# Turning the expert tokens on VectorE instead of TensorE, and loading w_down in blocks of whole rows, in a hybrid encoder layer with sixteen experts

## The reference

```python
aff = softmax(tok @ router_w)                 # tok: (512, 1024) of one sequence, 16 experts
gate, idx = lax.top_k(aff.T, 64)              # each expert takes its 64 best tokens
xs = tok[idx]
hid = silu(xs @ w_gate[e]) * (xs @ w_up[e])   # w_gate, w_up: (1024, 1408) for each expert
ye = (hid @ w_down[e]) * gate                 # w_down: (1408, 1024)
out = zeros.at[idx].add(ye)                   # added to the tokens' residual
```

## Time and profile before

| what | value |
|---|---|
| median of three runs | 1491.75 us (1491.37 to 1493.68) |
| profiled execution, from first to last instruction | 1489.4 us |
| mean granted TensorE clock | 0.996 |
| TensorE, VectorE, ScalarE, GpSimd busy | 99%, 80%, 55%, 11% of the span |
| the expert stage | about 712 to 1478 us |
| one expert, from block 0 to the next block 0 | 47.8 us |

### The profile page before, as it was taken

The page is one execution under the profiler, slowest core; times in us unless marked ns, Lnnn a source line. Parts: engine busy times, 40 slices in busy tenths (PEclk is TensorE's granted clock), DMA queues, the critical chain, the costliest instruction groups (busy, mean ns, idle before and its releaser), DMA issues.

```text
span 1489.4 us, 18913 instructions
## 1 busy us (share of the span) xinstructions
PE 1467.0 (99%) x7042; PEld 1235.5 (83%) x7042; DVE 1189.5 (80%) x1024; ACT 819.8 (55%) x777; POOL 167.3 (11%) x119
## 2 busy tenths in 40 slices
PE   9999999999999999998999999999999999999996
PEld 8878888888888888888888888888888888888885
DVE  5688988896767766346888888888888888888886
ACT  6322232123622222333677777777777777777776
POOL 1000001000005200011110112011110121012101
PEclk9999999999999999999999999999999999999998
DMA  7210232623263255677999999999999999999997
GB/s 236 58 43 0 81 87 75 224 85 99 94 230 121 87 183 197 227 253 283 347 362 365 376 376 374 384 374 377 374 377 381 377 374 374 384 376 376 374 374 286
DMA packets 220971, 388.26 MB, mean 261 GB/s; under 512 B 8603, under 2 KB 87771, under 8 KB 220412
## 3 DMA queue, kind: packets, MB, share of 16 engines
q1 hardware_dynamic: 213692, 361.39, 68.4%
q0 software_dynamic: 7232, 26.22, 5.8%
HBM read 348.78 MB, written 38.80 MB: 260 GB/s over the span
## 4 chain that ended last, share of the span: by engine, by line
PE 71%; DVE 2%; DMA 0%; issue 0%; ACT 0%; POOLq 0%; POOL 0%; ACTq 0%
PE ps L1779 23%; PE ps L1781 22%; PE ps L1780 22%; PE ps L2162 1%; PE ps L2154 1%; PE ps L2199 1%; PE ps L2082 0%; PE ps L2064 0%; DMA slot_tokens<-tok_rows,rows_to_gather 0%; DVE top_index L1651 0%; DVE affinity_rows L1654 0%; DVE top_of_halves L1647 0%; DVE expert_lo L1207 0%; DVE tok_rows L1592 0%; ACT expert_hi L804 0%
## 5 line engine op out<-in xcount | busy, mean ns | idle before, releaser
L1207 DVE TENSOR_TENSOR expert_lo<-expert_raw,expert_hi 128x2048 fp32r<-128x2048 f32 (+1 forms) x285 | 597.5, 2110 | 92.1 <-ACT expert_hi L804 91.1
L804 ACT ACTIVATE expert_hi<-expert_raw 128x2048 fp32r<-128x2048 f32 (+1 forms) x285 | 506.5, 1778 | 177.8 <-PE ps L1781 174.0
L1779 PE MATMUL ps<-expert_hi,slot_tokens_T_hi 128*128 128x512 f32 (+1 forms) x768 | 289.8, 377 | 2.0 <-DVE slot_tokens_T_lo L1207 1.0
L1780 PE MATMUL ps<-expert_lo,slot_tokens_T_hi 128*128 128x512 f32 (+1 forms) x768 | 285.2, 371 | 0.0
L1781 PE MATMUL ps<-expert_hi,slot_tokens_T_lo 128*128 128x512 f32 (+1 forms) x768 | 285.2, 371 | 0.0
L1779 PE MATMUL ps<-hT_hi,w_hi 128*128 128x512 f32 x576 | 226.2, 393 | 1.0 <-DVE hT_lo L1219 1.0
L1781 PE MATMUL ps<-hT_hi,w_lo 128*128 128x512 f32 x576 | 224.3, 389 | 0.0
L1780 PE MATMUL ps<-hT_lo,w_hi 128*128 128x512 f32 x576 | 224.2, 389 | 0.0
L1779 PEld LDWEIGHTS ps<-expert_hi,slot_tokens_T_hi 128*128 128x128 f32 x768 | 144.1, 188 | 25.1 <-issue 4.0
L1781 PEld LDWEIGHTS ps<-expert_hi,slot_tokens_T_lo 128*128 128x128 f32 x768 | 144.2, 188 | 20.4
L1241 DVE SCALAR_TENSOR_TENSOR conv_sum<-a_padded,small_params,conv_sum 128x1024 f32<-128x1024 f32 x120 | 158.1, 1317 | 3.4
(11 more groups left out here) (314 smaller groups left out, 1843.6 us busy)
## 6 DMA issues: line engine op xcount, KB each, us to landing
expert_raw<-in_w_gate SPq DMA_DIRECT2D x64, 1024.0 KB, 8.7
expert_raw<-in_w_up SPq DMA_DIRECT2D x64, 1024.0 KB, 8.6
expert_raw<-in_w_down SPq DMA_DIRECT2D x64, 1024.0 KB, 8.1
expert_raw<-in_w_gate SPq DMA_DIRECT2D x32, 768.0 KB, 7.5
expert_raw<-in_w_up SPq DMA_DIRECT2D x32, 768.0 KB, 7.2
expert_raw<-in_w_down SPq DMA_DIRECT2D x32, 768.0 KB, 8.5
w_raw<-in_w_in SPq DMA_DIRECT2D x36, 512.0 KB, 4.8
gate_in<-gate_spill SPq DMA_DIRECT2D x22, 512.0 KB, 3.9
```

The source lines that it names most:

```text
L804: nc.scalar.activation(out, src, ACT.Copy, **scale).then_inc(s, 1)
L1207: V.tensor_tensor(out, src, high_part.bitcast(F32), ALU.subtract).then_inc(s, 1)
L1779: nc.tensor.matmul(out, a[0], b[0], start=first, stop=False)
L1780: nc.tensor.matmul(out, a[0], b[1], start=False, stop=False)
```

## The change

It has four parts.

1. **Tokens of experts 1 to 15.** The gather becomes four indirect DMAs of a quarter row (256 channels) each; the row numbers differ by quarter of the partitions, from a new table `PIECES` made once in the routing stage (four small ScalarE copies, four small TensorE transposes, one VectorE operation, four more VectorE memsets earlier). VectorE then turns `XS` with one transpose of 128x1024 in squares of 32, reading every eighth element, into the new buffer `TURNED` after its part of block 8 (`turn_tokens`). ScalarE's high part comes ahead of its part of block 0 and waits until block 15 of the expert before has been used. The low part is made by GpSimd (`tokens_low`). The eight TensorE transposes stay for expert 0 alone.
2. **Row order.** The channels of a tile are now every eighth, so gate and up are loaded with eight neighbouring rows in a partition instead of rows 128 apart. The pieces stay 2 KB or 1.5 KB long.
3. **`w_down`.** A block is two row tiles with all 1024 columns. Blocks 10, 11, 16, 17 keep their size; 4 and 5, equal before, become 128x2048 and 128x1024. TensorE goes through both column halves tile by tile. `gate_out` waits for both blocks.
4. **Order elsewhere.** The load of the last norm's weights moves from the routing stage to the end of the weight loads. GpSimd's `scatter` of an expert comes one turn later in its program, after the gather of the expert after next.

```diff
 def src_of(kind, c, k, e):
     if kind == "down":
-        tiles = n // P
-        return w_down[bass.ds(e, 1), a:a + n, k * 512:(k + 1) * 512].rearrange(
-            "o (t p) n -> p (o t) n", p=P), tiles, 512
+        tiles, _ = place_of(kind, c, k)
+        a += 2 * k * P
+        return w_down[bass.ds(e, 1), a:a + tiles * P, :].rearrange("o (t p) n -> p (o t) n", p=P), tiles, D
     w = w_gate if kind == "gate" else w_up
-    return w[bass.ds(e, 1), k * 4 * P:(k + 1) * 4 * P, a:a + n].rearrange(
-        "o (t p) n -> p (o t) n", p=P), 4, n
+    return w[bass.ds(e, 1), :, a:a + n].rearrange(
+        "o (p t) n -> p (o t) n", p=P)[:, 4 * k:4 * k + 4, :], 4, n
 def place_of(kind, c, k):
-    return (n // P, 512) if kind == "down" else (4, n)
+    return (min(2, n // P - 2 * k), D) if kind == "down" else (4, n)
...
+            sp.wait_ge(xsT_lo, E)
+            sp.dma_start(NGF[:], norm_f_g.to_broadcast([P, D])).then_inc(norm_g_in, 16)
             sp.wait_ge(added, 16 * (E - 1))
...
 def gather(e):
+    pool.wait_ge(xs_in, (e - 1) * 64 + 16)
+    ge(pool, xs_turned, e)
+    pool.wait_ge(slots_ready, 5)
+    nc.gpsimd.tensor_copy(NEXT_PIECES[:], PIECES[:, bass.ds(e, 1), :].rearrange("p o a -> p (o a)")).then_inc(rows_next, 1)
     pool.wait_ge(x2_mm, WO_DONE)
     pool.wait_ge(rows_next, e)
-    pool.indirect_dma_start(XS[:], None, tok_dram,
-                            bass.IndirectOffsetOnAxis(ap=NEXT_ROWS[:], axis=0)).then_inc(xs_in, 16)
+    for a in range(4):
+        pool.indirect_dma_start(XS[:, a * 256:(a + 1) * 256], None, tok_pieces,
+                                bass.IndirectOffsetOnAxis(ap=NEXT_PIECES[:, a:a + 1], axis=0)).then_inc(xs_in, 16)
+def tokens_low(e):
+    pool.wait_ge(xsT_hi, e + 1)
+    nc.gpsimd.tensor_tensor(XST[1][:].rearrange("p k n -> p (k n)"), TURNED[:].rearrange("p k n -> p (k n)"),
+                            XST[0][:].rearrange("p k n -> p (k n)").bitcast(F32), ALU.subtract).then_inc(xsT_lo, 1)
...
-            with pool.Fori(1, E - 1) as e:
+            with pool.Fori(2, E - 1) as e:
+                tokens_low(e)
                 gather(e + 1)
-                scatter(e)
+                scatter(e - 1)
...
 def xsT_high(e):
-    act.wait_ge(xsT_mm, e + 1)
-    high(XST[0][:].rearrange("p k n -> p (k n)"), PS[:, 6:8, :].rearrange("p a n -> p (a n)"), xsT_hi)
+    act.wait_ge(xs_turned, e + 1)
+    act.wait_ge(e_used, e * NB - SKIPPED - len(down_units(1)))
+    high(XST[0][:].rearrange("p k n -> p (k n)"), TURNED[:].rearrange("p k n -> p (k n)"), xsT_hi)
 def act_body(e, base, first, last=False):
     for n in range(NB):
+        if n == 0 and not first:
+            xsT_high(e)
         if not (first and LEAD <= n < LEAD + SKIPPED) and not (last and n == NB - 1):
             split_e(n, e, base)
...
+def turn_tokens(e):
+    dve.wait_ge(xs_in, e * 64 + 16)
+    dve.wait_ge(xsT_lo, e)
+    V.transpose(TURNED[:], XS_BY_TILE).then_inc(xs_turned, 1)
+TURN_AT = 8
 def dve_body(e, base, first, last=False):
     for n in range(NB):
...
-        if n == (1 if first else 0):
-            xsT_low(e)
+        if first and n == 1:
+            first_tokens_low()
...
+        if n == TURN_AT and not last:
+            turn_tokens(e + 1)
...
 def pe_body(e, base, first, last):
...
     else:
-        tokens_of(e + 1)
         down(1, e, down_counts(1, e, base))
+        hidden_T(2, e)
         pe.wait_ge(xsT_lo, e + 2)
-        hidden_T(2, e)
```

More of the change, by code:

```diff
@@ L1087, in split_e @@
                 q = pos_mod(n, e, SPLITS)
-                high(ES[q][:, 0:tiles, 0:width], EW[r][:, 0:tiles, 0:width], e_hi)
+                high(block_of(ES[q], *BODY[n]), block_of(EW[r], *BODY[n]), e_hi)
             def silu(c, e, base):
@@ L1120, in gate_out @@
                     act.wait_ge(slots_ready, 3)
-                    act.wait_ge(e_used, used + dh)
+                    act.wait_ge(e_used, used + 1)
                     ge(act, added, e * 16)
@@ L1134, in act_body @@
                             nc.scalar.activation(LISTS[:, g, 0, :], TOP[32 * g:32 * g + E, :], ACT.Copy).then_inc(rows_ready, 1)
-                    if n == (2 if first else 0):
+                    if first and n == 2:
+                        act.wait_ge(pair_ready, 1)
+                        for a in range(4):
+                            part = nc.scalar.activation(FOUR_TIMES[:, a, :, :], PAIR[:, 1, 32 * a:32 * a + 32][:, None, :].to_broadcast([E, 4, P // 4]),
+                                                        ACT.Copy)
+                        part.then_inc(rows_ready, 1)
+                    if first and n == 2:
                         xsT_high(e)
@@ L1567, in _ @@
                 steps.did(V.memset(HALF_START[32 * g:32 * g + 32, :], float(H * g)))
+                steps.did(V.memset(QUARTER[32 * g:32 * g + 32, :], float(g)))
             def row_scale(t):
@@ L2148, in _, with slot_pieces @@
             nc.tensor.transpose(PS[:, 0, 0:E], PAIR[:, 0, :], IDENT[0:E, 0:E]).then_inc(slots_mm, 1)
+            def slot_pieces():
+                pe.wait_ge(rows_ready, 6)
+                for a in range(4):
+                    mm = nc.tensor.transpose(PS[:, 4, a * E:(a + 1) * E], FOUR_TIMES[:, a, :, :].rearrange("e b n -> e (b n)"),
+                                             IDENT[0:E, 0:E])
+                mm.then_inc(slots_mm, 1)
             def tokens_of(e):
@@ L2224, in pe_body @@
                     hidden_T(2, e)
-                    down_whole(HIDT_WHOLE, 4, 1, E * NB - SKIPPED - 1, False)
+                    landed(E * NB - SKIPPED - 1)
+                    for dh in range(2):
+                        for tile in (2, 3):
+                            mm = down_whole(HIDT_WHOLE, tile, dh, E * NB - SKIPPED - 1, 1, 1, False)
+                    mm.then_inc(e_used, 1)
                 else:
-                    tokens_of(e + 1)
                     down(1, e, down_counts(1, e, base))
+                    hidden_T(2, e)
                     pe.wait_ge(xsT_lo, e + 2)
-                    hidden_T(2, e)
             keep_busy(22)
+            slot_pieces()
             tokens_of(0)
@@ L2239, in _ @@
             pe.wait_ge(hidT_hi, NF * E + 1)
+            end_tiles = (F - 2 * 512) // P
+            for pair in range(2):
+                landed(E * NB - SKIPPED + pair)
             for dh in range(2):
-                down_whole(HIDT_END, (F - 2 * 512) // P, dh, E * NB - SKIPPED + dh, True)
+                for tile in range(end_tiles):
+                    mm = down_whole(HIDT_END, tile, dh, E * NB - SKIPPED + tile // 2, NF - 1, tile // 2, tile == end_tiles - 1)
+                mm.then_inc(e_used, 1)
 def kernel(**inputs):
```

104 lines of the change are left out of this document (57 added, 47 removed).

## The result

The changed kernel takes **1523.13 us** (median of 4 runs, 1522.92 to 1523.22) against 1491.89 us for the kernel before on the same chip (4 runs): ratio 1.0208, 95% interval 1.0193 to 1.0222, so 31 us slower. The forecast was 1502.8 us, in a range of 1484 to 1521. The sign was right. The size was nearly three times too small, and the range missed it by 2 us.

What follows compares the result with a forecast made beforehand. The prediction took TensorE's queue (99% busy) as the bound. It summed 15 x (-0.31 + 0.30 + 0.64) = +9.5 us and +1.5 us once to +11.0 us on 1491.75: 1502.8 us, range 1484 to 1521 us.

Steps and rivals of the forecast that it cites:

- Block 16: Removing the eight TensorE transposes ahead of block 16 saves 0.31 us per expert, 15 times, not their full 0.80.
- Block 0: GpSimd's subtraction holds up VectorE's low part of block 0, so TensorE loses 0.30 us per expert, 15 times.
- Block 9: Later low parts plus VectorE's transpose delay TensorE at block 9: 0.64 us lost per expert, 15 times.
- the shift by block 4: Block 4 with 12 matmuls instead of 9 delays ScalarE's parts of blocks 7 and 8 by 0.46 us.
- The upper bound (2.44 us): Longest assumed VectorE transpose ahead of block 9: two passes of 1.22 us, losing 1.86 us there.
- rival (c): VectorE's transpose ahead of block 9 takes two passes: +29.3 us, 1521.0 us; chance 0.13.
- its 19 us more: With the skill page's 2.49 us for VectorE's transpose, block 9 loses 1.91 us and the whole takes 19 us more.
- What occurs once: Single costs such as routing-stage work and the first gather: 0 to 3 us, taken as 1.5 us.
- Rival (d): Gathers land late, or the new row order slows the loads by over 5%: from 1510 us up; chance 0.07.
- Rival (a): VectorE fits both new operations in its gaps, leaving only the 0.31 us saving: 1488.6 us; chance 0.22.
- gives nothing back: VectorE's subtraction of 1024 columns after block 0 saves nothing when removed, as VectorE ran ahead of TensorE there.
- the lag that the prediction named: Loads need 48.6 us per expert against 47.8 us for one expert; the ring covers 12 us of lag.

Runs made afterwards that it cites:

- run 2: Changed kernel with the tokens' low part made by VectorE after its part of block 17, no GpSimd subtraction; 1514.4 us.
- run 3: Changed kernel with w_down in the old blocks (half the columns, all row tiles); 1516.3 us.
- run 4: Changed kernel with VectorE's transpose reading neighbouring elements instead of every eighth; does not compute the layer; 1508.5 us.
- run 11: Changed kernel with one gather of whole rows per expert instead of four of quarter rows; does not compute the layer; 1517.5 us.
- run 5: Changed kernel with VectorE's transpose after block 12 instead of 8 and the tokens' low part on VectorE after block 17, none on GpSimd; 1487.0 us.
- run 7: Kernel before with only w_down's new blocks of two row tiles of 1024 columns; 1491.5 us.
- run 1: Changed kernel with VectorE's transpose after its part of block 12 instead of block 8; 1495.8 us.
- run 8: Kernel before with one TensorE token transpose instead of eight per expert from the second on; does not compute the layer; 1490.9 us.
- run 9: Kernel before with w_down's new blocks, one token transpose, unturned tokens read from SBUF, TensorE's wait for their low part behind the hidden state's transposes; 1489.9 us.
- run 6: Changed kernel with the transpose after block 12, the tokens' low part on VectorE, and w_down's old blocks; 1492.4 us.

## Why the prediction was off, point by point

- **Block 16, right.** Forecast -0.31 us. From block 9 to block 16 it is now 1001.90 + 49.43 - 1033.91 = 17.42 us, before 1036.39 - 1018.64 = 17.75: -0.33. TensorE stands 0.17 us there; the forecast said about 0.3.
- **Block 0, right in kind, short in size.** Forecast +0.30. From block 16 to block 0 it is 6.70 us against 6.22: +0.48. GpSimd's subtraction holds VectorE as in the earlier trace rows, and the hold was sized right: TensorE starts block 0 4.56 us after VectorE's low parts of blocks 16 and 17 end (1008.60 - 1004.04), the forecast said 4.53. The 0.18 us short are mostly that block 16 now comes 2.35 us after the start of its low part instead of the 2.50 of the forecast. Run 2 without the subtraction gives 0.59 back.
- **Block 9, the step that failed.** Forecast +0.64, measured 1.66 + 0.33 - 0.48 = +1.51. Of its two terms the shift by block 4 was right (0.46; run 3 shows 0.52). The other, "I take 1.22 us, one pass at the pace of the subtraction", was mis-sized: 2.17 us. Run 4 shows that the pace itself was right, 1.24 us when neighbours are read. What was left out is that `XS_BY_TILE` reads every eighth element, which stands in the diff. Putting 2.17 for 1.22 in the same sum gives +1.59, close to what was measured. The upper bound (2.44 us) held the value; rival (c), priced from it, comes to 1521.0 us, but for a reason that did not occur: there are no two passes whatever the step. That the time came out near this rival is luck.
- **The rule of the Trainium skill** that was weighed there ("VectorE: DVE Perf Modes", section "The three transpose paths", 2.49 us for eight, an estimate by the page) was nearer to the trace's 2.17 us than the row chosen, and its 19 us more would have given 1521.8 us. But it says nothing of the step, and with step one the transpose takes 1.24 us (run 4), half of the estimate: that it came near is luck as well. For TensorE's transposes the same section's 390 ns stands against 0.10 us each here.
- **What occurs once**, forecast 1.5 us: 4.3 at the first expert, -0.5 in the tail and 3.3 at the end, 7.1 us. The late first gather had been named ("its transpose may wait once") but not priced, the lower clock behind it not at all, and the end not thought of. Run 11 shows 3.6 us of the first expert and the 3.3 us at the end to come with the four gathers.
- The sum: 15 x 1.66 + 7.1 = 32.0 us against 15 x 0.63 + 1.5 = 11.0. Of the 21 us missing, 15 x 0.87 = 13 hang on block 9, 15 x 0.18 = 2.7 on block 0, and 5.6 on what occurs once; block 16 gave 0.3 more than forecast.
- **Rival (d)** did not occur from the second expert on: VectorE waits for a gather once. No run tests the row order of gate and up alone, but with it the transfers go at 382 GB/s (run 5) and without it at 384 (run 7), so it does not slow them by 5%. **Rival (a)** asked for a transpose under 0.6 us; the runs show another way to free block 9, a place in the queue where a long one is covered (run 1).
- Of the removed VectorE operation the prediction said that it "gives nothing back: it stood where VectorE ran ahead of TensorE". The reason is wrong: in the kernel before it ended 0.13 us before TensorE's next step that needed it (run 8). It gave nothing back in the changed kernel because block 0 waits there for its own low part behind GpSimd's hold. What its place alone is worth no run isolates; run 5, where it comes ahead of block 0's part, is 0.46 us per expert shorter than run 9, where it comes behind.

That TensorE was 99% busy made its work look like the price list. Run 8 shows that it was not: 0.7 us of it per expert were cover for a chain of VectorE that is as long. The change pays when that chain is put in another order too (run 5), and then the loads have to keep up as well (run 6): the lag that the prediction named, 48.6 us against 47.8, grows with a shorter expert.

## What to carry to other kernels

When work moves to an engine that is nearly full, ask in which gap of its queue it lands: the same 2.1 us transpose cost 24 us over 15 experts ahead of a late block and next to nothing four blocks on. Price an operation with its access pattern, not only with its size. And before counting on time taken off the busiest engine, look for the chain that ends next; here TensorE's work, VectorE's low parts and the loads came one closely behind the other.

## What the runs showed of the hardware that was not expected

- A VectorE transpose of 128x1024 fp32 takes 1.24 us when it reads neighbours (run 4) and 2.17 us when it reads every eighth element.
- SyncE's last wait for TensorE's queue is 5.4 us with four gathers per expert (5.6 in run 6) and 2.1 us with one. Why it follows their number is not known; no run tries two or three.
- TensorE's granted clock fell (0.57 from 736 to 740 us, at the 1.2 GHz level for most of it) behind an idle time of 3.18 us, and stayed at 1.00 in run 11 where the wait at the same place was 1.05 us. The length of the idle time is not all that counts: run 2 stood 3.09 us there and stayed at 1.00, run 4 stood 2.19 us and fell to 0.58 from 734 to 738 us. Run 2, then run 4:

```profile
736.28 0.50 PE L1817 MATMUL ps<-expert_hi,slot_tokens_T_hi 128*128 128x512 f32 x1 [3.09 <-DVE expert_lo L1230]
...
736.00:740.00 4.00, 3.72 (x16) 2.90 (x17) 4.00 (x4) 0.61 (x1) 3.12 (x2) 1.00 1.05 401
```

```profile
734.26 0.50 PE L1818 MATMUL ps<-expert_hi,slot_tokens_T_hi 128*128 128x512 f32 x1 [2.19 <-DVE expert_lo L1238]
...
734.00:738.00 4.00, 3.74 (x10) 2.92 (x11) 4.00 (x4) 0.56 (x2) 0.00 (x0) 0.58 1.00 369
```

- With w_down in rows of 4 KB the stage's transfers went mostly at 381 to 384 GB/s in runs 5 and 7, with rows of 2 KB at 375 to 377 GB/s in run 6 and the kernel before.
- GpSimd took 1.00 us to issue a gather at 717.56 and 2.41 us at 723.88, in the same kernel; why is not known.
